# Six of twelve modulation units computed as scaled sums on GpSimd instead of as products on TensorE

## The reference

```python
c_act = jax.nn.silu(c)
mod = (c_act @ w_mod[l] + b_mod[l])[:, None, :]
sh1, sc1, gt1, sh2, sc2, gt2 = jnp.split(mod, N_MOD, axis=-1)
h = layer_norm(x) * (1.0 + sc1) + sh1
y = hybrid_mixer(h, ...)
x = layer_norm(DEEPNORM_ALPHA * x + (1.0 + gt1) * y, ln1_g[l], ln1_b[l])
h = layer_norm(x) * (1.0 + sc2) + sh2
y = hierarchical_moe(h, ...)
```

## Time and profile before

| what | value |
|---|---|
| median of three runs | 2143.76 us |
| the profiled execution | 2143.5 us |
| its span | 2141.7 us |
| mean granted TensorE clock | 0.873 |
| TensorE busy | 1616.5 us (75%) |
| VectorE busy | 419.9 us (20%) |
| ScalarE busy | 283.1 us (13%) |
| GpSimd busy | 60.3 us (3%) |
| moved by DMA | 670.53 MB, mean 313 GB/s |

### The profile page before, as it was taken

One profiled execution on the slowest core, in us unless ns is written; L12 is line 12 of the kernel. 1 busy time (PEld: TensorE's weight loads), 2 busy tenths in 40 slices (PEclk: granted clock), 3 DMA queues, 4 the chain that ended last, 5 costly groups with the idle time before them and its releaser, 6 DMA issues.

```text
span 2141.7 us, 19636 instructions
## 1 busy us (share of the span) xinstructions
PE 1616.5 (75%) x8021; PEld 829.8 (39%) x8021; DVE 419.9 (20%) x912; ACT 283.1 (13%) x632; POOL 60.3 (3%) x79
## 2 busy tenths in 40 slices
PE   6999999899998999999999644664365545545545
PEld 3774654344442677686644311311131111211111
DVE  5521642432213122121325200000000000000001
ACT  6211222110001222121233100000000000000000
POOL 2000000000000100111100000000000000000000
PEclk9999999989999999999999767877787777777777
DMA  9999332849997642344527499999999999999996
GB/s 354 336 365 348 105 100 79 343 164 421 427 428 293 225 176 100 133 143 138 175 75 287 197 428 428 428 427 429 427 428 427 428 427 428 427 428 428 427 428 265
DMA packets 104236, 670.53 MB, mean 313 GB/s; under 512 B 8227, under 2 KB 10984, under 8 KB 71120
## 3 DMA queue, kind: packets, MB, share of 16 engines
q1 hardware_dynamic: 100000, 657.63, 75.4%
q0 software_dynamic: 3712, 11.11, 1.6%
q10 hardware_dynamic: 432, 0.49, 0.1%
HBM read 661.86 MB, written 7.34 MB: 312 GB/s over the span
## 4 chain that ended last, share of the span: by engine, by line
PE 62%; DMA 32%; DVE 3%; ACT 2%; SPq 1%; issue 1%; DVEq 0%; ACTq 0%
PE psum L1099 14%; PE psum L1088 12%; DMA ring<-in_w_up 11%; DMA ring<-in_w_down 11%; PE psum L1695 10%; DMA ring<-in_w_gate 9%; PE psum L1434 5%; PE psum L1466 3%; PE psum L1351 2%; PE psum L1402 2%; PE psum L1054 2%; PE psum L1180 1%; PE psum L1473 1%; PE psum L1562 1%; SPq L786 1%
## 5 line engine op out<-in xcount | busy, mean ns | idle before, releaser
L1695 PE MATMUL psum<-work,prob 128*32 128x512 f32 x1024 | 290.9, 732 | 162.3 <-DMA ring<-in_w_up 87.2
L1695 PE MATMUL psum<-ring,prob 128*32 128x512 f32 x1024 | 291.0, 732 | 143.1 <-DMA work<-in_w_up 83.1
L1099 PE MATMUL psum<-ring,hT 128*128 128x512 f32 x672 | 306.3, 602 | 5.0 <-ACT hT L181 4.2
L1088 PE MATMUL psum<-hT,ring 128*128 128x256 f32 x1152 | 270.5, 381 | 1.6 <-ACT probT L181 0.8
L1088 PEld LDWEIGHTS psum<-hT,ring 128*128 128x128 f32 x1152 | 210.7, 190 | 36.2 <-issue 8.0
L1695 PE MATMUL psum<-work,hT 128*32 128x512 f32 x512 | 143.0, 721 | 82.7 <-DMA ring<-in_w_down 82.7
L1695 PE MATMUL psum<-ring,hT 128*32 128x512 f32 x512 | 143.0, 721 | 54.4 <-DMA work<-in_w_down 51.0
L1099 PEld LDWEIGHTS psum<-ring,hT 128*128 128x128 f32 x672 | 123.8, 193 | 138.6 <-issue 132.6
L1695 PEld LDWEIGHTS psum<-work,prob 128*32 128x32 f32 x1024 | 70.8, 131 | 267.2 <-issue 267.2
L1695 PEld LDWEIGHTS psum<-ring,prob 128*32 128x32 f32 x1024 | 71.0, 131 | 248.3 <-issue 247.3
L181 ACT ACTIVATE work<-psum 128x512 f32<-128x512 f32 (+2 forms) x99 | 57.0, 576 | 650.2 <-PE psum L1709 313.9
(11 more groups left out here) (334 smaller groups left out, 1430.0 us busy)
## 6 DMA issues: line engine op xcount, KB each, us to landing
work<-in_w_up SPq DMA_DIRECT2D x40, 2048.0 KB, 20.1
ring<-in_w_up SPq DMA_DIRECT2D x40, 2048.0 KB, 19.9
ring<-in_w_gate SPq DMA_DIRECT2D x38, 2048.0 KB, 18.8
work<-in_w_gate SPq DMA_DIRECT2D x38, 2048.0 KB, 19.6
work<-in_w_down SPq DMA_DIRECT2D x38, 2048.0 KB, 20.2
ring<-in_w_in SPq DMA_DIRECT2D x72, 1024.0 KB, 7.5
ring<-in_w_down SPq DMA_DIRECT2D x34, 2048.0 KB, 21.1
ring<-in_w_mod SPq DMA_DIRECT2D x24, 1024.0 KB, 12.5
```

The costliest lines, as they stand in the source:

```text
L1088: mm = pe.matmul(o[:, wide(j * S, S)], w[:, ch], actT[:, c, :], start=(c == 0), stop=(c == KC - 1))
L1099: mm = pe.matmul(o, lhs, w, start=(c == 0), stop=(c == KC - 1))
L1695: mm = pe.matmul(o[wide(i * CAP2, CAP2), :], lhs(chunks_per * piece + c, i), R.slot(l + i, (chunks_per, width))[:, c, wide(b * BANK, BANK) ...
```

## The change

Units 2 to 7 are no longer computed by `modulation`. Their weights come in parts of 0.5 MB (128 rows of 1024 numbers), issued by GpSimd on its own queue. GpSimd multiplies a part by a column of `cact` (tensor_scalar, one scalar per partition), and from the second part of a unit on adds it to the unit's sum (tensor_tensor). After 8 parts TensorE sums over the partitions with two products of 64 columns, zero but for one column (`add_partitions`). The products stand behind `xbc` chunk 3 (unit 2), `v` (unit 3), the first step of SSD's `y_diag` (unit 4) and steps 2, 8 and 14 of the fox attention (units 5, 6, 7). Units 8 and 9 move behind `z` chunks 0 and 1. `spread(2, 3)` moves behind the first merge product and `spread(4)` behind the last, and ScalarE takes them instead of VectorE. Two places hold sums in turn; parts go through three further places for units 2 to 4 and two for units 5 to 7. The load of a unit's first part waits until TensorE has finished the unit two before it. GpSimd starts when `hT_high` is complete, and its loads of `ln1_g` and the following ones now stand behind unit 7. SyncE's ring has 24 loads fewer, and from load 18 on it issues them behind the stores of bias groups 5 to 7 instead of between them. Before the first `assemble`, VectorE waits for the sum of unit 4.

```diff
-        IN_UNITS = dict(xbc=(2, 3, 4, 5), q=(6,), k=(7,), v=(8,), z=(9,))
+        IN_UNITS = dict(xbc={3: 2}, q={}, k={}, v={0: 3}, z={0: 8, 1: 9})
+        FOX_SUMS = {2: 5, 8: 6, 14: 7}
...
+        BESIDE_H = 3
+        part_places = [mod[:, 0, :], mod[:, 1, :], mod[:, 2, :], h[:, 0, :], h[:, 1, :], params[:, 1, :]]
+        part_in = [sem(f"unit_part_in{b}") for b in range(len(part_places))]
+        unit_parts = []
+        for i, u in enumerate(POOL_UNITS):
+            streams = (2, 3, 4) if i < BESIDE_H else (2, 5)
+            at0 = 0 if i < BESIDE_H else BESIDE_H
+            for c in range(KC):
+                unit_parts.append((u, c, streams[(7 * (i - at0) + c - 1) % len(streams)] if c else i % 2))
...
+            def fetch_part(n):
+                u, c, b = unit_parts[n]
+                if c == 0 and u >= POOL_UNITS[2]:
+                    pool.wait_ge(*done(job(f"unit{u - 2}")))
+                if b == 5 and all(place != 5 for _, _, place in unit_parts[:n]):
+                    pool.wait_ge(bias_stored[BIAS_STAGES - 1], BIAS_GROUPS // BIAS_STAGES * BIAS_STORES)
+                if c and step.last:
+                    pool.wait_ge(*step.last)
+                src = (w_mod, w_ada)[u // 6].rearrange("(p c) n -> p c n", c=KC)[:, c, wide(u % 6 * D, D)]
+                pool.dma_start(part_places[b], src).then_inc(part_in[b], 16)
+
+            def add_part(n):
+                u, c, b = unit_parts[n]
+                pool.wait_ge(part_in[b], 16 * len([m for m in range(n + 1) if unit_parts[m][2] == b]))
+                step(nc.gpsimd.tensor_scalar, part_places[b], part_places[b], cact[:, u // 6, c:c + 1], None, ALU.mult)
+                if c:
+                    step(nc.gpsimd.tensor_tensor, unit_sum(u), part_places[b], unit_sum(u), ALU.add, signals=unit_summed(u) if c == KC - 1 else None)
+
+            def place_free(n, added):
+                u, c, b = unit_parts[n]
+                before = [m for m in range(n) if unit_parts[m][2] == b]
+                return n <= added + 6 and (c == 0 or not before or before[-1] <= added)
+
+            pool.wait_ge(signal("cact_ready"), 1)
+            pool.wait_ge(signal("hT_high"), KC // 2)
+            fetched = 0
+            for n in range(-1, len(unit_parts)):
+                if n >= 0:
+                    add_part(n)
+                while fetched < len(unit_parts) and place_free(fetched, n):
+                    fetch_part(fetched)
+                    fetched += 1
...
+            def add_partitions(u):
+
+                o = begin(job(f"unit{u}"))
+                pe.wait_ge(*unit_summed(u))
+                for n in range(2):
+                    mm = pe.matmul(o[wide(64 * n, 64), :], one_column_at(u), unit_sum(u)[:, wide(n * BANK, BANK)], start=True, stop=True)
+                units_done.append(u)
+                end(mm)
...
-            spread(2, 3, 4)
...
+                if m == 0:
+                    add_partitions(4)
...
                 if i == 0:
+                    spread(2, 3)
...
+            spread(4)
             by_tile("mT", "w_o", h, "merged_ready")
...
+            for unit in (2, 3, 4):
+                for n in range(2):
+                    take(job(f"mod{unit}", n), mod[:, (2, 0, 1)[unit - 2], wide(n * BANK, BANK)], ACT.Identity, bias=0.0 if unit == 3 else 1.0)
...
+            add_row(3)
             add_row(8)
             add_row(9)
...
+            dve.wait_ge(*unit_summed(POOL_UNITS[BESIDE_H - 1]))
```

More of the change, by code:

```diff
@@ L364, in plan_spread, with plan_chunks @@
                 jobs(f"mod{u}", 2)
-        def plan_chunks(name, w, col0, n, units=(), first=0):
+        POOL_UNITS = range(2, 8)
+        def plan_chunks(name, w, col0, n, units={}, first=0):
             for i in range(first, n):
@@ L370, in plan_chunks @@
                 load_chunk(f"{name}_{i}", w, wide(col0 + i * BANK, BANK), job(name, 2 * i + 1))
-                if i < len(units):
+                if i in units and units[i] in POOL_UNITS:
+                    jobs(f"unit{units[i]}", 1)
+                elif i in units:
                     plan_unit(units[i])
@@ L396, in fill_span, with plan_attention @@
             return first, min(first + 2, (f + 1) * n // len(fills))
-        def plan_attention(name, n, fills, beside=()):
+        def plan_attention(name, n, fills, beside=(), sums={}):
             ends = {fill_span(f, fills, n)[1] - 1: fill for f, fill in enumerate(fills)}
@@ L414, in plan_attention @@
                     jobs(f"yT_{beside[i]}", 2)
+                if i in sums:
+                    jobs(f"unit{sums[i]}", 1)
             for fill in fills:
@@ L994, in build_program @@
         logits, in_group = sb("logits", [P, TT, 20]), rank
-        hot_g, hot1, hot2, e_in = sb("hot_g", [P, TT, 4]), sb("hot1", [P, TT, 4]), sb("hot2", [P, TT, 4]), sb("e_in", [P, TT, 4])
-        route_g = sb("route_g", [P, TT, 4])
+        hot_g = sb("hot_g", [P, TT, 4])
+        hot1, hot2, e_in, route_g = (row_max[:, wide(dil_unit0 + 4 * TT * i, 4 * TT)].rearrange("p (t e) -> p t e", t=TT) for i in range(4))
         @block.tensor
@@ L1102, in token_job, with add_unit, channel_major @@
                 finish(k, mm)
-            def channel_major(name, n, actT, units=(), first=0):
+            def add_unit(u):
+                if u in POOL_UNITS:
+                    add_partitions(u)
+                else:
+                    in_one(modulation(u))
+            def channel_major(name, n, actT, units={}, first=0):
                 for i in range(first, n):
@@ L1107, in channel_major @@
                         in_one(channel_job(name, i, half, actT))
-                    if i < len(units):
-                        in_one(modulation(units[i]))
+                    if i in units:
+                        add_unit(units[i])
             def by_tile(transposed, name, src, ready, between=()):
@@ L1119, in by_tile, with token_major @@
                         in_one(token_job(name, i, t, hT))
-            def token_major(name, n, actT, units=()):
+            def token_major(name, n, actT, units={}):
                 for i in range(n):
@@ L1135, in fill_job, with attention @@
                 return token_job(name, i, half, hT), KC
-            def attention(name, n, unit0, scores, values, keys, fills, beside=()):
+            def attention(name, n, unit0, scores, values, keys, fills, beside=(), sums={}):
                 shares = {}
@@ L2190, in _ @@
                          signals=(signal("conv_sum_ready"), ct + 1) if j == 3 else None)
-                if ct % 4 == 3:
+                if ct % 4 == 3 and ct // 4 in IN_UNITS["xbc"]:
                     add_row(IN_UNITS["xbc"][ct // 4])
@@ L2244, in _ @@
             step(v.tensor_tensor, a_exp[:, 1, :], bank(k)[:, 96:112], a_cs[:, 0, :], ALU.subtract, signals=emptied(k))
-            for unit in (2, 3, 4):
-                for n in range(2):
-                    k = job(f"mod{unit}", n)
-                    take(k, v.tensor_scalar, mod[:, (2, 0, 1)[unit - 2], wide(n * BANK, BANK)], bank(k), 0.0 if unit == 3 else 1.0, None, ALU.add)
             for j in range(4):
@@ L2328, in fox_mask @@
                 step(v.scalar_tensor_tensor, dst, src, neg_F[:, t, hd:hd + 1], causal[:, (1 - t) * P:2 * P], ALU.subtract, ALU.add, signals=taken)
[L2330 removed]
+            attention("fox", FOX_UNITS, 0, fox_mask, lambda i: i % TT + 1, lambda i: o_fox[:, i % TT, wide(i // TT * FOX_D, FOX_D)], fox_fills, beside=beside_fox)
             dve.wait_ge(signal("gates_ready"), 1)
@@ L2339, in _ @@
                     step(v.tensor_tensor, h[:, t, cols], h[:, t, cols], junk[:, 0:BANK], ALU.add, signals=(signal("merged_ready"), t + 1) if n else None)
+            for unit in (2, 3, 4):
+                for n in range(2):
+                    dve.wait_ge(*emptied(job(f"mod{unit}", n)))
             for j in range(4):
```

37 lines of the change are left out of this document (26 added, 11 removed).

## The result

The changed kernel takes 2188.95 us (median of 4 runs, 2187.22 to 2192.86), the kernel before 2143.21 beside it: ratio 1.0221, 95% interval 1.0206 to 1.0236. The profiled execution has a span of 2185.4 us. The direction was as predicted. The size was not: 2167 was predicted, with a range up to 2182.

A forecast was written before the change was run, and what follows sets the result against it. TensorE was taken to bound the first block and DMA the experts, first-block changes moving the end one to one. -16.1 + 19 + 8.5 + 8 + 3 + 1.3 = +23.7 on 2143.5 gave 2167 us, range 2133 to 2182.

The forecast's parts named there:

- Term one: TensorE's products: six units at 3.57 us replaced by column products at 0.88 each, -16.1 us.
- Term three: Inputs of `cumsum`: unit 9 loses its cover (+4.3) and small VectorE operations are hit (+4.2), +8.5 us.
- Term six: Moved spread: ScalarE takes `mod4` ahead of its table load and the token copies TensorE waits for, +1.3 us.
- a sign of being wrong: In the attention: TensorE waiting for GpSimd there would show the prediction wrong; no size given.
- Term two: Bias steps: sixteen convolution operations at 1.7 us beside GpSimd make the operands late, +19 us.
- Term four: SSD: VectorE's two-input operations are held by GpSimd in each later step, +8 us, bounds 0 and 15.
- The step that failed: GpSimd's multiplication in each part: assumed 1.3 us, between 0.95 and 2.36, making a part 4.5 us.
- The later tiles, 0: Convolution tiles ahead of `dtf_sum`: GpSimd pauses for unit 2's product, VectorE catches up, cost 0.
- if GpSimd has no such pause, up to 30: Later convolution tiles: without GpSimd's wait for unit 2's product, they cost up to 30 us.
- The attention, 0: Attention: units 5 to 7 taken without a wait, GpSimd's ten parts needing 42.3 us against 43.8 available.
- GpSimd as the bound: Attention: without the lock but with a 2.36 us scale, TensorE waits 6.4 at unit 7; 2141 us, chance 0.07.
- Term five: Clock: new gaps at the bias steps and `cumsum` bring TensorE work at half speed, +3 us (0 to 6).

The follow-up runs named there:

- broadcast form: Against the changed kernel, GpSimd's multiplication was written as a tensor_tensor with the condition's column broadcast along the row: 2170.86 us, ratio 1.0133.
- the two kernels with parts of about 4 us: Against the changed kernel, GpSimd multiplied whole parts but added only column 0 (2142.08 us), or the reverse (2866.59 us, with changed routing).
- the multiplication's: Against the changed kernel, GpSimd multiplied whole parts but added only column 0: 2142.08 us, ratio 1.0001.

## Why the prediction missed

**Right.** The change is slower because GpSimd's arithmetic and VectorE's share something that the one can hold against the other: one column instead of 1024 brings everything back (2136.86). That it is held for the whole instruction is so for GpSimd's tensor_tensor; its tensor_scalar holds VectorE's sums for its first 0.93 us only. Term one: -16.1, came -15.4 (1.01 per unit instead of 0.88). Term three: +8.5, came 9.8 with its clock. Term six: +1.3, came 1.5. What was named as a sign of being wrong, TensorE waiting for GpSimd in the attention, came true.

**Term two, the bias steps:** +19, came 13.3. Where both engines are dense, four operations fit one part of 6.23, so 1.55 us each instead of 1.7 in a part of 4.5. Over the sixteen operations ahead of the bias steps it was 1.19: they took 19.0 us (59.47 to 78.48) instead of 27.2, the first four of them 1.96, as alone, beside a multiplication (58.26 to 61.10) that was past its first microsecond. With the form that does not let VectorE through (broadcast) the wait was 18.66.

**Term four, SSD:** +8, came 9.0, and that is luck in part. The term was made of waits for VectorE, and these are 1.31, 1.61 and 0.85, together 3.8. The other 5.3 is TensorE's own work at a lower clock: the granted clock is 0.70 from 236 to 243 us, behind `cumsum`, and 0.65 from 292 to 301, where it was 1.00 in the same places before.

**The step that failed** is "I take 1.3, nearer to the memset, since it reads one stream and not two". The multiplication took 2.87, above even the upper bound, for which an instruction with two inputs had been taken. A part was 6.23 and not 4.5 us. Two zeros hung on that number, and they hold where a part is short: in the two kernels with parts of about 4 us both waits are absent.
- *The later tiles, 0.* Thirteen parts from 55.2 us on, two of them without an addition, end at 130 with the measured prices, and the issue behind them at 130.7, when unit 2's product (129.87) is just done: GpSimd waited 0.53, VectorE did not catch up, and `dtf_sum` cost 15.0. The prediction named this case ("if GpSimd has no such pause, up to 30") but gave it no chance. The broadcast form, with a part of 5.24, shows it from the other side: a pause of 22.9 us, and no wait at `dtf_sum`. (The 115 us at which the prediction lets GpSimd stand still don't follow from its numbers: 48 and 13 times 4.5 are 106.5. With a part of 4.5 the pause is there either way.)
- *The attention, 0.* When unit 5's product came (306.40), GpSimd was still in a part of unit 6, and behind it had two parts of that unit and the eight of unit 7. It was through at 370.24, 63.8 us later, and unit 7's place was 48.6 behind unit 5's product: a wait of 15.2 by that sum, 15.39 measured. The prediction's room, 43.8, was too small: it took step 3 of the attention to start at 290.94, but in the trace before it is this row:

```profile
282.97 0.70 PE L1325 MATMUL psum<-work 64*128 64x256 f32 x2
```

  Its own rival, GpSimd as the bound, had this mechanism. In the right room and with the measured price its sum gives 3.4 + 9 x 6.23 - 48.6 = 10.9 of the wait; the rest is the part that GpSimd was still in. With a price of 2.36 it gives 50.2 - 48.6 = 1.6, and the broadcast form, with a part of 5.24, had no wait at all. The prediction had that rival only in a world without the lock, and it was true beside the lock.

Of the 45.7 us at the gather, 29.7 stand at these two places (15.0 and 14.7), for which the sum had nothing. All other places together came to +16.0, against the predicted +23.7. So the lock was real, but too dear at the bias steps and put at nothing for the later tiles; GpSimd's pace was real too, and put at nothing in the attention. The range's upper end (2182) had put a dear multiplication only into the lock's terms.

**Term five, the clock:** +3, came about 10: 3.5 at `dtf_sum`, 1.1 at `cumsum` and 5.3 in SSD, all within the numbers above. This term was mis-sized as well.

**What stays open.** Why GpSimd's tensor_scalar of one input is slower than its tensor_tensor, and that again slower than the same with a broadcast operand, was not settled; a scalar from SBUF is excluded (0.09). Why sums of VectorE pass a tensor_scalar of GpSimd after its first microsecond is not shown either. A fused multiply and add on GpSimd was not tried.

## What to carry to other kernels

An engine whose price for an operation isn't in the trace is not bounded by its neighbours' prices; ask first at which price a zero in the sum stops being one, and put that into the range. "Idle" GpSimd is not free room: in these traces VectorE's two-input instructions waited for it where it read SBUF, and the fast one-input ones also where it only wrote, so its work belongs where VectorE's is not next on the path. With half of its work left out, and 1.2 to 1.5 us between its long instructions in each part, the loss at the gather, against one column, was 8.7 and 7.5 us instead of 53.2; such gaps with the whole work were not tried. If such a sum is worth doing off TensorE, try VectorE first: here 1.28 us per 128x1024 part instead of 6.23, and 2136.06 instead of 2188.95 us.

## What the runs showed of the hardware

- GpSimd, 128x1024 in 32 bits: tensor_scalar 2.85 to 2.87 us (2.78 with an immediate), tensor_tensor 2.35, tensor_tensor with one operand broadcast from a column 1.91, memset 0.965. The Trainium skill, "GPSIMD Engine Reference", section "Engine selection", has one-input operations at roughly line rate; the measured 2.87 stands against it.
- GpSimd's tensor_scalar of 2.85 us holds VectorE's sums (two inputs in SBUF) until 0.93 us after its start, in the changed kernel as in the multiplication's; sums that begin 1.3 us or more behind it take 0.48, as alone (14 of 14 up to 160 us in the changed kernel). VectorE's fast one-input operations that begin 1.5 to 2.0 us behind it get through only at 2.6, while one that began 1.2 behind it took 0.41, as alone. GpSimd's tensor_tensor lets a fast operation through only at about its end (2.25 for an operation of 0.41, with 2.09 left of GpSimd's).
- The lock is not symmetric in cost: in the rows above GpSimd's tensor_tensor went from 2.35 to 2.48 beside VectorE, and VectorE's operation from 0.41 to 2.25.
- A gap costs TensorE more than its length: 11.5 us of wait at `dtf_sum` came with 3.5 us lost to a lower clock.
